# Nine merge gates of an encoder layer computed in a stage of their own ahead of the first attention, four pairs of them by seven products

## The chip, the cores and the metric

One NeuronCore of a Trainium2 chip runs the whole program. The metric is the device time of one execution in microseconds, and lower is better. The engines are TensorE (PE in the profile), VectorE (DVE), ScalarE (ACT) and GpSimd (POOL). SyncE (SP) issues the DMAs.

## The reference

Two sequences of 512 tokens (1024 tokens together, 1024 features) go through one layer. Its merge is what the change touches (`mg` is the last 3 * 1024 columns of `u`):

```python
h = rms_norm(x, pre_g)
u = h @ w_in
ya = diff_attention(...) * silu(ag)
yb = gqa_attention(...) * silu(bg)
yc = neighbourhood_attention(...) * silu(cg)
gates = jax.nn.sigmoid(mg).reshape(b, s, 3, D_MODEL)
m = gates[:, :, 0] * (ya @ wa) + gates[:, :, 1] * (yb @ wb) + gates[:, :, 2] * (yc @ wc)
x = x + rms_norm(m @ w_out, post_g)
x = x + sigmoid(x @ w_pg) * (p_i @ w_pe)
```

The gates depend on h alone, so they may be computed at any time after h is there.

## The kernel before

Features lie on the partitions and tokens along the free axis. Every product is done in float32 with each operand split into a high and a low part (`_hi`, `_lo`) and three matmuls (hi by hi, hi by lo, lo by hi). The high part of a weight is cast by ScalarE (`split_w`, line 1598 of the profile). Its low part is the difference, which GpSimd takes (line 728).

The program goes through: normalising x and turning it into h; attention A; merge 0; attention B; merge 1; attention C; merge 2; the output projection; the embedding. A merge `b` works on eight chunks `f` of 128 output features. For every chunk there is a **gate**, a product of h with 128 columns of `w_gates` (48 matmuls of 512 columns), and a **branch**, a product of the attention's output y with a block of `w_branch` (24 matmuls). ScalarE takes the tanh of the gate from PSUM into `s_row(c)` (`merge_tanh`, line 1818), and VectorE multiplies it with the branch product and adds that to `m` (`merge_add`, `add_quarter`).

Chunks 0 and 1 of a merge are done plainly. From chunk 2 on the branch products of two chunks, 2p and 2p+1, are done together as **pair p**, with seven products in place of eight (Strassen's scheme in Winograd's form, six matmuls for each product: `pair_first` does four of them, 24 matmuls, and `pair_rest` three, 18 matmuls). Merge 2 does its last two chunks plainly. VectorE puts the seven products together (`pair`, lines 2357 and 2348 to 2351). GpSimd makes the sums of the weights in place in `stage` (lines 747 to 757).

The order on each engine is written out by hand. Semaphores count up: `w_ready` the weights whose low part is done, `block_done` the weights that TensorE has used up, `mg_tanh` the gates that have been through tanh, `merged` the chunks that have gone into `m`. An engine takes its instructions strictly in the order written. TensorE's order in a merge is gate 0, gate 1, branch 0, gate 2, branch 1, gate 3, and then for each pair

```python
pair_first(b, p, n + 4 * p + 2, slot)
merge_gate(b, 2 * p + 2, n + 4 * p + 3, 1 - slot, 0)
pair_rest(b, p, n + 4 * p + 4, slot)
merge_gate(b, 2 * p + 3, n + 4 * p + 5, 1 - slot, 1)
```

with the last pair of merges 0 and 1 without gates. `pair_first` begins with `pe.wait_ge(merged, LEAD + b * KC + 2 * p)`: both chunks of the previous pair must have gone into `m`.

Of the kernel before, what the change touches and what calls it, by code (L numbers as in the profile page):

```python
# [144 lines left out]
N_MERGE = [19, 42, 74]  # L145
PAIRS = [range(1, KC // 2), range(1, KC // 2), range(1, KC // 2 - 1)]
HALF_K = 2 * P
N_B = 35
N_C = 58
N_OUT = 90  # L150
EARLY = KC - 2
N_PG = [N_OUT + 2, N_OUT + KC + 4]
N_PE = N_OUT + KC + 2

# [7 lines left out]
def build_program(nc, w_qkvg_a, w_qg_b, w_qkvg_c, w_gates, w_branch, w_out, w_pg, w_pe,  # L162
# [3 lines left out]
    with ExitStack() as ctx:  # L166
# [17 lines left out]
        m = sb("m", [P, TILES, KC, P])  # L184
# [9 lines left out]
        pt_lo = sb("pt_lo", [P, 2, QT, SEQ], F32R)  # L194
# [35 lines left out]
        x_in = [sem(f"x_in{i}") for i in range(TILES)]  # L230
# [99 lines left out]
        xr_in = [sem("x_again0"), sem("x_again1")]  # L330
        mt_hi_done = sem("mt_hi_done")
        mt_ready = sem("mt_split")
        out_w_in = [sem(f"w_out_in{k}") for k in range(EARLY)]
# [18 lines left out]
        o_stored = [sem("stored0"), sem("stored1")]  # L352
# [24 lines left out]
        FIRST_BANKS = {("q", 0): 4, ("k", 0): 5, ("q", 1): 0, ("k", 1): 1}  # L377
# [164 lines left out]
        def _(sp):  # L542
# [11 lines left out]

            def load_merge_rest(b):
                n = N_MERGE[b]
                for f in range(2):
                    load_w(n + 2 + 2 * f, n % 2, w_branch[b * KC + f])
                    load_w(n + 3 + 2 * f, (n + 1) % 2, w_gates[b * KC + 2 + f])
                for p in PAIRS[b]:  # L560
                    sp.wait_ge(w_ready, LEAD + n + 4 * p + 1)
                    pair = w_branch[b * KC + 2 * p:b * KC + 2 * p + 2].rearrange("a p n -> p a n")
                    sp.dma_start(stage[:, n % 2, :].rearrange("p (a n) -> p a n", a=2), pair) \
                        .then_inc(w_in_slot[n % 2], 16)
                    if p < KC // 2 - 1:
                        load_w(n + 4 * p + 3, (n + 1) % 2, w_gates[b * KC + 2 * p + 2])
                        sp.wait_ge(w_ready, LEAD + n + 4 * p + 3)
                        sp.sem_inc(w_in_slot[n % 2], 16)
                        load_w(n + 4 * p + 5, (n + 1) % 2, w_gates[b * KC + 2 * p + 3])
                    else:  # L570
                        sp.wait_ge(w_ready, LEAD + n + 14)
                        sp.sem_inc(w_in_slot[(n + 1) % 2], 16)
                        sp.wait_ge(w_ready, LEAD + n + 16)
# [10 lines left out]
            def load_x(t):  # L584
                sp.dma_start(x_row(t), x_tok[t]).then_inc(x_in[t], 16)
# [7 lines left out]
            sp.wait_ge(x_in[2], 16)  # L593
# [15 lines left out]
            for c in range(2):  # L609
                sp.sem_inc(o_stored[c], LEAD)  # L610
# [7 lines left out]
            for n in range(2, 4):  # L618
                load_w(N_A + n, n % 2, w_qkvg_a[N_A + n])
# [7 lines left out]
            load_w(N_KQV + 2, 0, w_qkvg_a[N_KQV + 2])  # L627

# [38 lines left out]
            for k in range(EARLY):  # L667
                sp.dma_start(out_early[k], w_out[k]).then_inc(out_w_in[k], 16)
# [4 lines left out]
            for c in range(2):  # L673
                sp.dma_start(y[:, c, :], x_tok[c]).then_inc(xr_in[c], 16)
# [23 lines left out]
            for c in range(2):  # L698
                sp.wait_ge(o_stored[c], LEAD + 16 * TILES)
# [3 lines left out]
        def _(pool):  # L703
# [18 lines left out]
            def split_w(n, slot, dst=None, width=TOK, hi=None, staged=None):  # L722
# [2179 lines left out]
```

## Time and profile before

| what | value |
|---|---|
| runs listed | 1332.16, 2647.54 and 3365.67 us |
| median of them | 2647.54 us |
| profiled execution: span | 1330.3 us |
| fastest listed run, the one that belongs beside this span | 1332.16 us (1.9 us more than the span) |
| instructions in the trace | 17488 |
| TensorE busy | 1312.1 us, 99% |
| VectorE, ScalarE, GpSimd busy | 680.8, 575.5, 352.0 us |
| HBM read and written | 66.86 and 4.23 MB |

An execution with this span cannot have taken 2647 us, so the profile describes the fastest of the three. Matmuls are pipelined: a matmul of 512 columns is shown with 0.39 us, but the next one starts 0.23 us behind it, so durations of groups in the chain of work are used, not the mean of one matmul.

### The profile page before, as it was taken

The numbers are of one execution on the slowest core, as the hardware profiler recorded it, in microseconds if no ns is written. First come the engines' busy times: TensorE is split into PE (matmuls) and PEld (weight loads), VectorE is DVE, ScalarE is ACT, GpSimd is POOL, SyncE is SP. The second block draws the span as 40 slices with busy tenths as digits, with TensorE's granted clock in tenths as the row PEclk, the third lists the DMA queues.
The fourth block names the chain that finished last, engine by engine and source line by source line (L and its number), as shares of the span: only waits on it lengthen the run. The fifth ranks groups of instructions, "written<-read, shape, count | busy, mean of one in ns | idle before, by whom it ended". The sixth has DMA issues, their size and how long they took to land.

```text
span 1330.3 us, 17488 instructions
## 1 busy us (share of the span) xinstructions
PE 1312.1 (99%) x6636; PEld 1072.0 (81%) x6636; DVE 680.8 (51%) x1285; ACT 575.5 (43%) x1106; POOL 352.0 (26%) x239
## 2 busy tenths in 40 slices
PE   8999999999999999999999999999999999999998
PEld 6788877888888778788888888888877888888887
DVE  6354655556522677786633435555557337435222
ACT  6355455553222577676422245555554223223210
POOL 4122212222434311130244512221211443213100
PEclk9999999999999999999999999999999999999999
DMA  6111112111111200000111211111001114422111
GB/s 214 63 41 41 46 36 57 52 32 52 49 48 32 67 30 16 17 20 21 52 52 32 81 61 33 51 51 42 32 24 41 48 40 167 140 81 70 58 40 40
DMA packets 25712, 72.18 MB, mean 54 GB/s; under 512 B 2808, under 2 KB 4728, under 8 KB 25504
## 3 DMA queue, kind: packets, MB, share of 16 engines
q1 hardware_dynamic: 25632, 71.09, 16.9%
q8 instruction: 53, 0.87, 0.3%
q14 instruction: 27, 0.22, 0.1%
HBM read 66.86 MB, written 4.23 MB: 53 GB/s over the span
## 4 chain that ended last, share of the span: by engine, by line
PE 90%; DVE 4%; ACT 3%; issue 1%; DMA 1%; POOL 1%; SPq 0%; ACTq 0%; DVEq 0%; POOLq 0%
PE ps L934 18%; PE ps L953 14%; PE ps L1290 13%; PE ps L1548 7%; PE ps L1528 6%; PE ps L1175 5%; PE ps L1342 5%; PE ps L1331 2%; PE ps L973 2%; PE ps L1112 2%; PE ps L1028 2%; PE ps L1260 2%; PE ps L1554 2%; PE ps L1406 2%; PE ps L1143 1%; PE ps L1234 1%
## 5 line engine op out<-in xcount | busy, mean ns | idle before, releaser
L728 POOL TENSOR_TENSOR w_lo<-stage,w_hi 128x1024 fp32r<-128x1024 f32 (+2 forms) x84 | 190.3, 2265 | 577.5 <-ACT w_hi L1598 577.5
L1598 ACT CAST w_hi<-stage 128x1024 fp32r<-128x1024 f32 (+2 forms) x92 | 91.3, 992 | 198.0 <-PE ps L934 125.9
L2148 DVE TENSOR_TENSOR pt_lo<-ps,pt_hi 128x512 fp32r<-128x512 f32 (+2 forms) x160 | 97.1, 607 | 80.6 <-ACT pt_hi L1962 40.3
L953 PE MATMUL ps<-h_hi,w_hi 128*128 128x512 f32 x272 | 110.3, 405 | 0.0
L934 PE MATMUL ps<-h_hi,w_hi 128*128 128x512 f32 x352 | 108.9, 391 | 0.7 <-POOL w_lo L728 0.7
L934 PE MATMUL ps<-h_lo,w_hi 128*128 128x512 f32 x352 | 108.5, 389 | 0.0
L934 PE MATMUL ps<-h_hi,w_lo 128*128 128x512 f32 x352 | 108.4, 389 | 0.0
L1290 PE MATMUL ps<-h_hi,w_hi 128*128 128x512 f32 x256 | 106.8, 417 | 0.0
L953 PE MATMUL ps<-h_hi,w_lo 128*128 128x512 f32 x272 | 106.2, 391 | 0.0
L953 PE MATMUL ps<-h_lo,w_hi 128*128 128x512 f32 x272 | 106.1, 390 | 0.0
L1290 PE MATMUL ps<-h_hi,w_lo 128*128 128x512 f32 x256 | 100.5, 392 | 0.0
L1290 PE MATMUL ps<-h_lo,w_hi 128*128 128x512 f32 x256 | 100.3, 392 | 0.0
L709 POOL TENSOR_TENSOR small<-small 128x1 f32<-128x1 f32 (+3 forms) x32 | 34.2, 1067 | 174.2 <-DVE small L2163 173.5
L934 PEld LDWEIGHTS ps<-h_hi,w_hi 128*128 128x128 f32 x352 | 65.6, 188 | 15.1 <-issue 1.8
L934 PEld LDWEIGHTS ps<-h_hi,w_lo 128*128 128x128 f32 x352 | 66.1, 188 | 13.8
L934 PEld LDWEIGHTS ps<-h_lo,w_hi 128*128 128x128 f32 x352 | 66.1, 188 | 13.8
L953 PEld LDWEIGHTS ps<-h_hi,w_hi 128*128 128x128 f32 x272 | 51.1, 188 | 15.1 <-issue 5.4
L1627 ACT ACTIVATE s<-s,stat 128x512 f32<-128x512 f32 x64 | 45.8, 716 | 38.0 <-DVE stat L2199 38.0
L1175 PE MATMUL ps<-h_hi,w_hi 128*128 128x512 f32 x144 | 59.8, 415 | 0.5 <-POOL w_lo L728 0.5
L953 PEld LDWEIGHTS ps<-h_hi,w_lo 128*128 128x128 f32 x272 | 51.1, 188 | 11.2
L953 PEld LDWEIGHTS ps<-h_lo,w_hi 128*128 128x128 f32 x272 | 51.2, 188 | 9.3
L2470 DVE CUSTOM_DVE_ANT_0 s<-ps,tables_plain 128x256 f32<-128x256 f32 (+1 forms) x64 | 29.0, 489 | 56.2 <-PE ps L1234 51.9
(386 smaller groups left out, 3059.3 us busy)
## 6 DMA issues: line engine op xcount, KB each, us to landing
stage<-in_w_gates SPq DMA_DIRECT2D x24, 512.0 KB, 3.6
stage<-in_w_qkvg_a SPq DMA_DIRECT2D x19, 512.0 KB, 4.4
stage<-in_w_qkvg_c SPq DMA_DIRECT2D x16, 512.0 KB, 3.6
m<-in_x_tok SPq DMA_DIRECT2D x8, 512.0 KB, 6.4
stage<-in_w_branch SPq DMA_DIRECT2D x8, 512.0 KB, 3.7
y_plain<-in_x_tok SPq DMA_DIRECT2D x8, 512.0 KB, 3.7
stage<-in_w_pg SPq DMA_DIRECT2D x16, 256.0 KB, 3.0
out<-y_plain SPq DMA_DIRECT2D x16, 256.0 KB, 2.0
```

Of the source, the lines that this page charges most:

```text
L709: nc.gpsimd.tensor_tensor(dst, src, neg_half.broadcast_to([P, n]), ALU.pow).then_inc(signal, 1)
L728: nc.gpsimd.tensor_tensor(dst, stage[:, staged, 0:width], f32(hi), ALU.subtract).then_inc(w_ready, 1)
L934: done = mm(ps[:, bank + g, :], w[:, slot, k * P:(k + 1) * P], h[:, k, g * SEQ:(g + 1) * SEQ], start=first and part == 0, stop=last and pa ...
L953: done = mm(ps[:, half_bank(T), :], w[:, slot, k * P:(k + 1) * P], h[:, k, g * SEQ:(g + 1) * SEQ], start=k == 0 and part == 0, stop=k == K ...
L1175: done = mm(ps[:, bank_b(name, unit, g), :], w[:, slot, k * P:(k + 1) * P], h[:, k, g * SEQ:(g + 1) * SEQ], start=k == 0 and part == 0, st ...
L1290: done = mm(ps[:, bank, :], w[:, slot, k * P:(k + 1) * P], h[:, k, g * SEQ:(g + 1) * SEQ], start=k == 0 and part == 0, stop=k == KC - 1 an ...
L1342: done = mm(ps[:, bank, :], w[:, slot, cols], h[:, c, :], start=c == 0 and part == 0, stop=c == 1 and part == 2)
L1528: done = mm(ps[:, 2 * c + nb, :], a[:, k * P:(k + 1) * P], w[:, k, nb * 512:(nb + 1) * 512], start=k == 0 and part == 0, stop=k == KC - 1 ...
L1548: mm(ps[:, c, :], a[:, k * P:(k + 1) * P], w[:, k * 512:(k + 1) * 512], start=k == 0 and part == 0, stop=k == KC - 1 and part == 2)
L1598: nc.scalar.copy(dst, stage[:, staged, 0:width]).then_inc(w_hi_done, 1)
L1627: done = nc.scalar.activation(probs, probs, ACT.Exp, bias=stat[:, T % 2, 2 + e:3 + e], accum_out=stat[:, T % 2, 4 + e:5 + e])
L2148: sub = lambda out, whole, hi: nc.vector.tensor_tensor(out, whole, f32(hi), ALU.subtract)
```

## The change

The odd gates from 3 to 7 of the three merges, nine of 24, move into a stage of their own, between the first projections and attention A. Gate 3 of merge 0 is done plainly (`plain_gate`, two halves of 24 matmuls). The other eight form four pairs, each done by seven products of 12 matmuls (`gate_product`). The sums of h that the scheme needs are made once: two of the four whole copies by GpSimd, all the rest by VectorE. ScalarE casts the high parts and takes the tanh. Each quarter of a gate pair, 128 by 512, is stored to DRAM (`gate_scratch`), and the merge loads the row of 128 by 1024 back into `s_row(1)` when it needs it (`load_gate_row`).

In a merge the order on TensorE becomes gate 0, gate 1, branch 0, branch 1, gate 2, and then for each pair `pair_first`, gate 2p+2, `pair_rest`. The core of the diff (`merge` is ScalarE's part, `gate_w_sums` and `gate_adds` are VectorE's):

```diff
+            def load_gate_row(b, f):
+                sp.wait_ge(merged, LEAD + b * KC + f - 1)
+                sp.dma_start(s_row(1), gate_scratch[b * KC + f]).then_inc(row_in[1], 16)
...
             def load_merge_rest(b):
...
                 if KC // 2 - 1 not in PAIRS[b]:
                     for f in range(2):
-                        load_w(n + 14 + f, (n + f) % 2, w_branch[b * KC + 6 + f])
+                        load_w(n + 11 + f, (n + 11 + f) % 2, w_branch[b * KC + 6 + f])
+                    load_gate_row(b, 7)
+                    sp.wait_ge(w_ready, LEAD + n + 12)
+                    sp.sem_inc(w_in_slot[(n + 11) % 2], 16)
...
             def merge_rest(b):
-                merge_gate(b, 2, n + 3, 1 - slot, 0)
-                merge_branch(b, 1, n + 4, slot)
-                merge_gate(b, 3, n + 5, 1 - slot, 1)
+                merge_branch(b, 1, n + 3, (n + 1) % 2)
+                merge_gate(b, 2, n + 4, n % 2, 0)
                 for p in PAIRS[b]:
...
-                        merge_gate(b, 2 * p + 2, n + 4 * p + 3, 1 - slot, 0)
-                        pair_rest(b, p, n + 4 * p + 4, slot)
-                        merge_gate(b, 2 * p + 3, n + 4 * p + 5, 1 - slot, 1)
+                        merge_gate(b, 2 * p + 2, at + 1, 1 - slot, 0)
+                        pair_rest(b, p, at + 2, slot)
...
+            def gate_product(J, product):
+                a, a22 = G_A1, G_A22[J % 2]
+                (s2s4, s3s1) = G_S
+                (hi, lo), first, state = {P1: (a, 0, "11"), P2: (a, SEQ, "21"), P3: (s2s4, SEQ, "22"), P6: (s2s4, 0, 2),
+                                          P7: (s3s1, 0, 3), P5: (s3s1, SEQ, 1), P4: (a22, 0, 4)}[product]
+                gate_bank_free(7 * J + product)
...
+                for c in range(QT):
+                    cols = slice(first + c * P, first + (c + 1) * P)
+                    for part, (w, h) in enumerate([(hi, 0), (hi, 1), (lo, 0)]):
+                        done = mm(ps[:, g_bank(J, product), :], w[:, cols], G_STATE[state][h][:, c, :],
+                                  start=c == 0 and part == 0, stop=c == QT - 1 and part == 2)
...
+            plain_gate(0)
             first_product("q", 1, range(KC))
             first_product("k", 1, range(KC))
+            plain_gate(1)
+            for J in range(N_PAIRS):
+                for product in range(7):
+                    gate_product(J, product)
+            pe.wait_ge(g_added, 7 * N_PAIRS - 4)
             half_step(-2, lambda T: None)
+            pe.wait_ge(g_tanh, GROUPS + 4 * N_PAIRS)
             score_pair(0)
...
             def merge(b):
-                split_w(n + 3, 1 - slot, uses(3))
                 merge_tanh(b, 1, n + 1, 1)
-                split_w(n + 4, slot, uses(4), width=512)
+                split_w(n + 3, (n + 1) % 2, uses(n + 3), width=512)
+                split_w(n + 4, n % 2, uses(n + 4))
...
-                split_w(n + 5, 1 - slot, uses(5))
-                merge_tanh(b, 2, n + 3, 0)
+                merge_tanh(b, 2, n + 4, 0)
                 for p in PAIRS[b]:
                     pair(p)
...
+            def gate_w_sums(J):
+                a11, a12, a21, a22 = [G_RAW[J % 2][:, q * SEQ:(q + 1) * SEQ] for q in range(4)]
+                steps.done(dve, nc.vector.tensor_tensor(a22, a21, a22, ALU.add))
+                nc.vector.tensor_tensor(a21, a11, a21, ALU.subtract)
+                steps.done(dve, nc.vector.tensor_tensor(a11, a22, a11, ALU.subtract))
+                nc.vector.tensor_tensor(a12, a12, a11, ALU.subtract).then_inc(gw_summed, 1)
...
+            for J in range(N_PAIRS):
+                gate_adds(J)
```

Three places show how the rows move.

**TensorE, merge 1, where pair 1 ends and pair 2 begins.** Before, the last six matmuls of the pair (line 1342) are followed by gate 5 (line 934):

```order
L1342 MATMUL ps<-pt_hi,w_hi 128x512 [waits second_partial_saved]
L1342 MATMUL ps<-pt_lo,w_hi 128x512
L1342 MATMUL ps<-pt_hi,w_lo 128x512
L1342 MATMUL ps<-pt_hi,w_hi 128x512
L1342 MATMUL ps<-pt_lo,w_hi 128x512
L1342 MATMUL ps<-pt_hi,w_lo 128x512
L934 MATMUL ps<-h_hi,w_hi 128x512 [waits w_split,merge_tanh_done]
L934 MATMUL ps<-h_hi,w_hi 128x512
L934 MATMUL ps<-h_lo,w_hi 128x512 x2
```

In the changed kernel the same six (now line 1454) are followed at once by the first product of pair 2, which waits for `merged`:

```order
L1454 MATMUL ps<-pt_hi,w_hi 128x512 [waits second_partial_saved]
L1454 MATMUL ps<-pt_lo,w_hi 128x512
L1454 MATMUL ps<-pt_hi,w_lo 128x512
L1454 MATMUL ps<-pt_hi,w_hi 128x512
L1454 MATMUL ps<-pt_lo,w_hi 128x512
L1454 MATMUL ps<-pt_hi,w_lo 128x512
L1454 MATMUL ps<-pt_hi,w_hi 128x512 [waits w_split,merged]
L1454 MATMUL ps<-pt_lo,w_hi 128x512
L1454 MATMUL ps<-pt_hi,w_lo 128x512
L1454 MATMUL ps<-pt_hi,w_hi 128x512
```

Gate 5, 48 matmuls, has gone from between them.

**ScalarE, merge 1, from the sums of y to the weights of pair 1.** Line 1861 (2026 after) casts the sums, the 128x1024 casts of line 1598 (1766) are high parts of weights, line 1818 (1986) is a tanh and line 1831 (2000) belongs to pair 1. Before:

```order
L1861 CAST y<-y_plain 128x2x512
L1861 CAST q_hi<-q_lo_plain 128x1024
L1598 CAST w_hi<-stage 128x1024 [waits block_done,stage1_in]
L1818 ACTIVATE s<-ps 128x1024 [waits merged,block_done]
L1598 CAST w_hi<-stage 128x1024 [waits block_done,stage0_in]
L1831 CAST pt_hi<-k_hi_plain 128x512 x2
L1834 CAST w_hi<-stage 128x256 [waits weight_sums_done]
```

In the changed kernel:

```order
L2026 CAST y<-y_plain 128x2x512
L2026 CAST q_hi<-q_lo_plain 128x1024
L1986 ACTIVATE s<-ps 128x1024 [waits merged,block_done]
L1766 CAST w_hi<-stage 128x1024 [waits block_done,stage1_in]
L2000 CAST pt_hi<-k_hi_plain 128x512 x2
L2003 CAST w_hi<-stage 128x256 [waits weight_sums_done]
```

The cast of gate 3's weights is gone from ahead of the tanh of gate 2, so that the tanh stands next ahead of the cast of pair 1's weights, as before, but with no other gate on TensorE behind gate 2.

**SyncE, the end of merge 2.** Before, the loads of the output projection's weights (line 668) follow the two last blocks of `w_branch`:

```order
L563 DMA stage<-in_w_branch 128x2x512 [waits w_split]
L546 DMA stage<-in_w_gates 128x1024 [waits w_split] x2
L546 DMA stage<-in_w_branch 128x512 [waits w_split] x2
L668 DMA y_plain<-in_w_out 128x1024 [waits max_ready,state_sums_done,y_written,y_split]
L668 DMA y_plain<-in_w_out 128x1024 x3
L668 DMA vg_plain<-in_w_out 128x1024
L668 DMA tables_plain<-in_w_out 128x1024
```

In the changed kernel the load of a gate row (line 619) has come between, and waits for `merged`:

```order
L607 DMA stage<-in_w_gates 128x1024 [waits w_split]
L619 DMA s<-gate_scratch 128x1024 [waits merged]
L607 DMA stage<-in_w_branch 128x512 [waits w_split] x2
L619 DMA s<-gate_scratch 128x1024 [waits merged]
L777 DMA y_plain<-in_w_out 128x1024 [waits w_split,max_ready,state_sums_done,y_written,y_split]
L777 DMA y_plain<-in_w_out 128x1024 x3
L777 DMA vg_plain<-in_w_out 128x1024
```

## Rows read from the trace of the kernel before

**Rows 1.** The page: busy time and share of TensorE, and its granted clock.

```profile
PE 1312.1 (99%) x6636; PEld 1072.0 (81%) x6636; DVE 680.8 (51%) x1285; ACT 575.5 (43%) x1106; POOL 352.0 (26%) x239
...
PEclk9999999999999999999999999999999999999999
```

**Rows 2.** Waits of TensorE: total us, times, longest.

```profile
PE ps L1112 <- DVE pt_lo L2148: 2.8, 8, 0.6
...
PE ps L934 <- POOL w_lo L728: 0.7, 1, 0.7
```

**Rows 3.** Chain that ended last, in merges 0 and 1: start, us, what.

```profile
357.57 10.88 PE ps L934 x48
368.45 5.44 PE ps L1342 x24
...
384.77 4.13 PE ps L1342 x18
388.90 10.89 PE ps L934 x48
...
664.37 10.88 PE ps L934 x48
...
691.57 4.08 PE ps L1342 x18
695.65 10.88 PE ps L934 x48
```

**Rows 4.** Timeline of ScalarE, merge 0, around the weights of pair 1: start, us, what.

```profile
353.18 1.02 ACT L1818 ACTIVATE s<-ps 128x1024 f32<-128x1024 f32 x1
357.66 1.05 ACT L1598 CAST w_hi<-stage 128x1024 fp32r<-128x1024 f32 x1 [3.47 <-PE ps L1331]
...
362.37 0.41 ACT L1834 CAST w_hi<-stage 128x256 fp32r<-128x256 f32 x1 [2.61 <-POOL stage L748]
```

**Rows 5.** Timeline of GpSimd at the same weights, merge 0 and (last row) merge 1.

```profile
358.79 2.40 POOL L747 TENSOR_TENSOR w_lo<-stage,w_hi 128x1024 fp32r<-128x1024 f32 x1 [3.04 <-ACT w_hi L1598]
361.26 1.07 POOL L748 TENSOR_TENSOR stage<-stage 128x256 f32<-128x256 f32 x1
362.92 0.74 POOL L751 TENSOR_TENSOR w_lo<-stage,w_hi 128x256 fp32r<-128x256 f32 x1 [0.59 <-ACT w_hi L1834]
...
670.25 1.17 POOL L751 TENSOR_TENSOR w_lo<-stage,w_hi 128x256 fp32r<-128x256 f32 x1 [0.58 <-ACT w_hi L1834]
```

**Rows 6.** Timeline of VectorE behind pair 1 of merge 0.

```profile
390.99 1.88 DVE L2348 SCALAR_TENSOR_TENSOR m<-s,ps 128x512 f32<-128x512 f32 x3
```

**Rows 7.** Timeline of VectorE behind pair 1 of merge 1.

```profile
698.49 1.34 DVE L2351 TENSOR_TENSOR m<-m,s 128x512 f32<-128x512 f32 x1
...
701.79 0.69 DVE L2351 TENSOR_TENSOR m<-m,s 128x512 f32<-128x512 f32 x1
```

**Rows 8.** Timelines of the end of merge 2: SyncE, ScalarE, TensorE.

```profile
1100.07 1.75 SPq L668 DMA_DIRECT2D y_plain<-in_w_out  x4
...
1112.48 3.88 ACT L2076 CAST h_hi<-y_plain 128x1024 fp32r<-128x1024 f32 x4
...
1121.66 0.62 PE L1528 MATMUL ps<-h_hi,q_hi 128*128 128x512 f32 x2
```

**Rows 9.** DMA issues between 1090 and 1140 us: median us to landing.

```profile
y_plain<-in_w_out SPq DMA_DIRECT2D x4, 512.0 KB, 7.3
```

**Rows 10.** Timelines of the first 30 us: VectorE and GpSimd.

```profile
19.09 1.28 DVE L2399 SCALAR_TENSOR_TENSOR m<-m,small,vg_plain 128x1024 f32<-128x1024 f32 x1
21.14 3.40 DVE L2399 SCALAR_TENSOR_TENSOR m<-m,small,vg_plain 128x1024 f32<-128x1024 f32 x1 [0.78 <-POOL small L709]
...
21.07 2.39 POOL L728 TENSOR_TENSOR w_lo<-stage,w_hi 128x1024 fp32r<-128x1024 f32 x1
```

**Rows 11.** Timeline of TensorE at the start of the program.

```profile
1.45 6.83 PE L920 MATMUL ps<-pt_hi 128*128 128x512 f32 x20 [1.45 <-DVE pt_hi L2150]
...
11.03 1.64 PE L920 MATMUL ps<-pt_hi 128*128 128x512 f32 x6
```

More of the change, by code:

```diff
@@ L153 @@
 N_PE = N_OUT + KC + 2
+GATE_PLAIN = (0, 3)
+GATE_PAIRS = [((0, 5), (0, 7)), ((1, 3), (1, 5)), ((1, 7), (2, 3)), ((2, 5), (2, 7))]
+N_PAIRS = len(GATE_PAIRS)
+GATE_RING = [6, 7, 4, 5, 0, 1, 2, 3]
+P1, P2, P3, P6, P7, P5, P4 = range(7)
+QUARTERS = [(0, 0), (1, 1), (0, 1), (1, 0)]
+GATE_SLOTS = 4
+GATES_STORED = [len(range(slot, GROUPS + 4 * N_PAIRS, GATE_SLOTS)) for slot in range(GATE_SLOTS)]
+TANHS = [0, 1, 2, 4, 6]
+ROWS_BACK = 9
 KEPT = 6
@@ L627, in _ @@
             load_w(N_KQV + 2, 0, w_qkvg_a[N_KQV + 2])
+            for slot in range(GATE_SLOTS):
+                sp.wait_ge(o_stored[slot], 16 * GATES_STORED[slot])
             sp.wait_ge(maxed, LEAD + TILES)
@@ L787, in _ @@
                 x_inv_sqrt(t)
+            pool.wait_ge(gw_hi_done, 1)
+            nc.gpsimd.tensor_tensor(G_PLAIN[1], stage[:, 0, :], f32(G_PLAIN[0]), ALU.subtract).then_inc(gp_ready, 1)
+            pool.wait_ge(h_ready, LEAD + QT)
+            for T, half in ((1, 0), (4, 1)):
+                hi, lo = h_quarter(half, 0)
+                nc.gpsimd.tensor_tensor(G_SUM[T], f32(hi), f32(lo), ALU.add).then_inc(gt_whole, 1)
             spread_bias(0)
@@ L1361, in pair_first, with pair_rest @@
                 pair_product(slot, 2 * HALF_K, T_PARTS[b][1], 3).then_inc(block_done, 1)
[L1363 removed]
+            def pair_rest(b, p, n, slot, count=1):
                 number = pair_number(b, p)
@@ L1393, in merge_rest, with plain_gate @@
                 if KC // 2 - 1 not in PAIRS[b]:
-                    merge_branch(b, 6, n + 14, slot)
-                    merge_branch(b, 7, n + 15, 1 - slot)
+                    merge_branch(b, 6, n + 11, (n + 11) % 2)
+                    merge_branch(b, 7, n + 12, (n + 12) % 2, count=2)
+            def plain_gate(g):
+                hi, lo = G_PLAIN
+                pe.wait_ge(gp_ready, 1)
+                if g == 0:
+                    pe.wait_ge(h_ready, LEAD + 6)
+                bank = [0, 3][g]
+                for k in range(KC):
+                    for part, (w, h) in enumerate([(hi, h_hi), (hi, h_lo), (lo, h_hi)]):
+                        done = mm(ps[:, bank, :], w[:, k * P:(k + 1) * P], h[:, k, g * SEQ:(g + 1) * SEQ],
+                                  start=k == 0 and part == 0, stop=k == KC - 1 and part == 2)
+                done.then_inc(gate_half, 1)
@@ new lines, in gate_adds @@
+            def gate_adds(J):
+                x0, x1 = G_X
+                more = J + 1 < N_PAIRS
+                bank = lambda product: ps[:, g_bank(J, product), :]
+                add = lambda out, in0, in1: nc.vector.tensor_tensor(out, in0, in1, ALU.add).then_inc(g_added, 1)
+                if more:
+                    gate_a22_lo(J + 1)
+                dve.wait_ge(g_p1_saved, J + 1)
+                dve.wait_ge(g_done, 7 * J + 2)
+                add(bank(P2), x0, bank(P2))
+                if more:
+                    gate_a1_lo(J + 1)
+                    gate_w_sums(J + 1)
+                dve.wait_ge(g_done, 7 * J + 4)
+                add(x0, x0, bank(P6))
+                if more:
+                    gate_sum_lo(J + 1, 0)
+                dve.wait_ge(g_done, 7 * J + 5)
+                dve.wait_ge(g_added, 7 * J + 2)
+                add(x1, x0, bank(P7))
+                dve.wait_ge(g_done, 7 * J + 6)
+                add(x0, x0, bank(P5))
+                dve.wait_ge(g_added, 7 * J + 3)
+                add(bank(P5), x1, bank(P5))
+                dve.wait_ge(g_added, 7 * J + 4)
+                add(bank(P3), x0, bank(P3))
+                dve.wait_ge(g_done, 7 * J + 7)
+                add(bank(P4), x1, bank(P4))
+                if more:
+                    gate_sum_lo(J + 1, 1)
@@ L2432, in _ @@
+            gate_sum_lo(0, 1)
+            gate_state_lo(1)
+            gate_state_lo(4)
+            for J in range(N_PAIRS):
+                gate_adds(J)
             dve.wait_ge(const_in, 16 * 3)
```

437 lines of the change are left out of this document (323 added, 114 removed).

## The prediction, made before the changed kernel ran

> **What bounds the kernel now.** I read the page first. TensorE is busy for 1312.1 of the 1330.3 us and its granted clock is full all along; no other engine is above 51% [rows 1]. Then the waits of TensorE: the largest sum is 2.8 us, and the only wait on a low part of a merge's weights is 0.7 us [rows 2]. So the kernel is a string of matmuls, and an edit is worth what it removes from the string or what gap it opens in it. Last I read the chain that ended last through merges 0 and 1. It is TensorE from end to end, gate and pair parts butted together: 10.88 us for a gate, 5.44 for 24 matmuls of a pair, 4.13 for 18 [rows 3]. That is 0.2267 us for a matmul of 512 columns. What the other engines do under each gate is then read in the timelines of ScalarE, GpSimd and VectorE.
>
> Of the runs listed, only 1332.16 fits the profiled span (1.9 us more). I make the sum against it; the median, 2647.54, is of executions that this profile does not describe. Two per cent, about what a measurement of this kernel can tell from no change, is 26.6 us.
>
> **Matmuls removed.** Nine gates of 48 matmuls are 432. In their place come one plain gate of 48 and four pairs of 7 x 12 = 84, together 384. 48 fewer at 0.2267 give **-10.9 us**. Two small waits go: the 0.7 us on GpSimd's low part [rows 2], whose weights get time while the new stage runs, and some 0.5 us (an estimate) where the first projections waited for the last of h, since the plain gate's first half needs less of it. Together **-12.1**.
>
> **The entrance of pair 1, three merges.** After the change TensorE has nothing between gate 2 and pair 1. What pair 1 needs is seen in merge 0: the cast of its weights on ScalarE (1.05 us at 357.66), GpSimd's low part 2.40, its sums 1.07, a cast of 0.41, GpSimd's 0.74, done at 363.66 [rows 4, 5]. Gate 3 ran from 357.57 to 368.45 [rows 3] and hid the 6.1 us. The order on ScalarE now puts the tanh of gate 2, 1.02 us [rows 4], ahead of that cast, and the tanh cannot begin before gate 2 has ended. So the wait is 6.1 + 1.0 = 7.1 us. In merge 1 the same chain ran from 664.37 to 671.42 [rows 3, 5], 7.05 without the tanh; GpSimd's short operations were longer there, beside VectorE's adds of branch 1. These adds now fall under gate 2, so I take 7.1 in all three: **+21.3**, with 18 and 24 as ends.
>
> **Behind `pair_rest`, six places.** `pair_first` of the next pair, and in merge 2 branch 6, waits until both chunks of the pair are in `m`. Before, the odd gate ran meanwhile. In merge 0 the matmuls of pair 1 ended at 388.90 [rows 3] and VectorE's last operation on it at 390.99 + 1.88 = 392.87 [rows 6]: 3.97 us. In merge 1 they ended at 695.65 [rows 3] and VectorE at 701.79 + 0.69 = 702.48 [rows 7]: 6.83, because gate products must be multiplied and then added to `m` instead of set. One add there took 1.34 where its like took 0.69 [rows 7], so 0.65 is a collision with GpSimd; GpSimd's work on the next weights will shift, and I take 6.2. Two waits of merge 0 at 4.0, two of merge 1 and two of merge 2 at 6.2: **+32.8**, ends 26 and 37. Nothing late behind these: the weights of the next pair need about the 6 us of rows 4 and 5, beginning when `pair_first` has freed their slot, and lie under the even gate.
>
> **The exit of merge 2.** SyncE issued the loads of the output projection at 1100.07 [rows 8], just as pair 2 ended; call that T. They landed 7.3 us later [rows 9]. ScalarE's four casts began at T + 12.4 and TensorE went on with the projection at T + 21.6 [rows 8], behind gate 7 and two branches, with no wait to speak of. Now the load of gate row 7 stands ahead of them in SyncE's queue and waits for `merged`, T + 6.2, and its 512 KB are in the same queue: four such loads took 7.3 [rows 9], so at most 1.8 for one; I take 1.4. The projection's loads land at T + 6.2 + 1.4 + 7.3 = T + 14.9. TensorE, without gate 7, is through both branches at T + 6.2 + 10.9 = T + 17.1. The first cast (1.0) and the low parts, of which VectorE did four in one run of some 4.6 us, with one more operation of about 1 us ahead of what TensorE needs, reach T + 21.5. That is a wait of 4.4, and for the load's own issue 0.4 each on SyncE (1.75 for four, [rows 8]) I take **+5**, ends 2 and 8.
>
> **The new stage.** Gates now go out to DRAM in 16 stores of 256 KB and come in again in 8 loads of 512 KB. A row is asked for when the pair before is in `m`, and used 5.4 + 10.9 + 4.1 = 20 us later [rows 3]; even the 7.3 us of rows 9 lie under that, so nothing. VectorE is the risk. Per pair it has 12 additions of 128x512 at 0.69 [rows 7] and three of 128x1024 at 1.22 to 1.28 [rows 10], 12 us, ScalarE 6.5, against 84 matmuls, 19.0 us: covered by 7 us. The first pair also needs the sums of h: some ten operations twice as wide as the 1.28 of rows 10, about 24 us, from 1.0 us after TensorE enters the stage until P3, which TensorE reaches after 120 matmuls, 27.2 us. If they run freely there is 2 us in hand. But a VectorE operation of 1.28 took 3.40 while GpSimd's of 2.39 ran [rows 10], and GpSimd makes two of the copies here: if the first sum is so held, VectorE is 4.4 us later and TensorE waits 2.3. I take **+1.5**, ends 0 and 20 (the upper end: each pair short by 5 us, where every 1024-wide addition meets GpSimd as in rows 10). The Trainium skill, "GPSIMD Engine Reference", in its table of the engine, says that GpSimd shares its SBUF interfaces with VectorE and that an instruction of VectorE with two SBUF inputs contends for them; by that the first sum is held and the wait is 2.3, without it 0.
>
> The sum so far: 1332.2 - 12.1 + 21.3 + 32.8 + 5 + 1.5 = **1380.7**.
>
> **How TensorE goes on after a gap.** The trace of before has no gap above 1.5 us, so it has no row for a restart but the start of the program: its first 20 matmuls took 6.83 us where 20 x 0.2267 is 4.5 [rows 11], and later ones have their usual rate. That is 2.3 us lost, though the granted clock of the page reads full in that slice too [rows 1]. Seven of the waits (three of 7.1, four of 6.2) are long; if each ends in such a restart, 7 x 2.3 = **+16.1**; the bounds are 0 and 7 x 2.3 with the two waits of 4 us as well, 20.7. I take 16.1, as the start of the program is the only gap of this length that I can see. The Trainium skill, "TensorE: Matmul & The Clock Gate", in its section on why this matters for kernels, says that an idle gap between bursts of matmuls puts the clock back to half of full speed, 1.2 of 2.4 GHz; by that rule each such wait would be paid for twice, which speaks against this change more than its own waits do. No wait of the trace can show it.
>
> The forecast is 1380.7 + 16.1 = **1397** (1396.8).
>
> **The rivals.**
> (1) *The waits without slow restarts*: matmuls run at full rate at once after a gap, 1381. For it: no gate in the chain shows such a price. Against it: none stands behind a long wait, and [rows 11] is the one stretch that does.
> (2) *The waits are short, the other side*: the chains behind gate 2 and behind `pair_rest` shrink, since VectorE and GpSimd work alone while TensorE stands still, and reading PSUM meets no matmuls. The place is the nine merge waits, the price their mean. The time is 1332.2 - 12.1 + 5 + 1.5 = 1326.6 plus nine waits; it stays under the 2% line at 1358.8 when they hold less than 32.2 us, 3.6 us each, against 6.0 by the rows. With 2.8 each it is 1352 (1351.8). With fully covered waits, were an order on an engine other than I read it, it would be 1321, the 10.9 us gained, which is also less than 2%. Against it: operations like 128x512 at 0.69 hold their length in every row without a collision.
> (3) *The new stage starves TensorE*: 20 us more as above, and four more slow starts at most: 1415 or so. For it: the 3.40 us row. Against it: GpSimd has little to do in the stage after the first pair.
> (4) *The change doesn't do what it says*: the order of the instructions shows that the nine gates left the merges, so this is nearly out.
>
> **How the numbers follow.** The forecast of 1397 has 0.50; rival 1 (1381) 0.27; rival 3 (1415) 0.10; rival 2 within 2% (about 1352) 0.11 with the covered case in it; faster by over 2%, under 1305.5, would need more than the 10.9 us that the matmuls can give, 0.02. The predicted time is 1397. Low end: rival 1 with the waits at their low ends (18 for 21.3, 26 for 32.8, 2 for 5) is 1367.6, 1368. High end: the forecast with its entrance and tail terms at 24 and 37 and the exit at 8 is 1407, and the larger restarts and part of rival 3 carry it to 1414. What is left out is rival 2 and half of rival 3, under 0.2. Chances: faster 0.02, same 0.11, slower 0.87.
>
> **What the changed profile would show.** The string of matmuls: 6488 instead of 6536 in all, and no gate between `pair_rest` and the next `pair_first`. The waits of TensorE: three of about 7 us on GpSimd's second low part, and six of 4 to 6.5 on VectorE's adds; if these are under 3.6 us on average, rival 2 holds. The first matmuls behind each: a group of 24 at 7.7 us instead of 5.44 shows the slow restart, 5.44 rival 1. In the exit: the six loads issued some 7 us after `pair_rest`'s end and a wait of about 5 before the output projection. In the new stage: a wait of 0 to 2.3 us ahead of the first P3 and none in later pairs; waits of several us in each pair show rival 3. I would be wrong outright if the weights of pair 1 or the adds were let go at another point than the orders show, or if the time between the new stage and attention A were not hidden by its last products.

## The result, and the profile after

The changed kernel takes 1412.49 us (median of four runs, 1411.8 to 1413.84). The ratio to the kernel before is **1.060** (95% interval 1.059 to 1.062). Left out of every comparison are executions far above the rest of their kernel: 2647.54 and 3365.67 us of the kernel before here, for which no clock is on record, and later one of 1449.52 us of that kernel and one of 1438.69 us of the first experiment's, both at a lower granted clock. The other two of the kernel before here are 1332.16 and 1332.57 us. The change is **80 us slower**. The forecast was 1397, 65 us slower, with a range from 1368 to 1414.

The page's engine line, the granted clock, and then the waits of TensorE in the changed kernel (who waits for whom: total us, times, longest), which answer to [rows 1, 2]:

```profile
PE 1325.7 (94%) x6588; PEld 1078.9 (77%) x6588; DVE 752.3 (53%) x1355; ACT 593.1 (42%) x1131; POOL 341.6 (24%) x233
...
PEclk9999999999999989999998989999999989999999
```

```profile
PE ps L1454 <- POOL w_lo L853: 21.0, 3, 7.0
PE ps L1454 <- DVE m_plain L2597: 18.8, 3, 6.4
PE ps L1443 <- DVE m_plain L2597: 7.1, 1, 7.1
PE ps L1285 <- POOL w_lo L837: 4.1, 2, 3.6
PE ps L1071 <- ACT s L1986: 4.0, 1, 4.0
PE ps L1454 <- DVE m_plain L2594: 4.0, 1, 4.0
PE ps L1044 <- POOL w_lo L837: 3.7, 1, 3.7
...
PE ps L1696 <- DVE m_plain L2556: 2.8, 1, 2.8
```

TensorE still has by far the most work, but it now stands still for 84.3 us of the span (1410.0 less 1325.7), 66 more than before (18.2), and the clock row has four 8s where it had only 9s. Three rows were forecast by name: the low part of pair 1's weights (three times 7.0), the adds of the pair before (18.8, 4.0 and 7.1 in five waits, and 4.0 where the third pair of merge 0 waits for a tanh), and the exit of merge 2 (2.8). Two were not: 3.6 and 3.7 us for a low part at L1285 and L1044, the first products of attentions B and C.

The chain that ended last, from the end of gate 2 of merge 0 into attention B (start, us, what):

```profile
435.70 10.89 PE ps L1044 x48
...
446.64 0.90 issue
447.54 1.05 ACT w_hi L1766
448.65 2.35 POOL w_lo L849
451.08 1.06 POOL stage L850
452.16 0.41 ACT w_hi L2003
452.71 0.73 POOL w_lo L853
...
453.58 7.04 PE ps L1454 x24
...
479.66 7.36 PE ps L1454 x24
...
508.01 11.10 PE ps L1454 x42
519.18 1.05 ACT w_hi L1766
520.31 2.36 POOL w_lo L837
522.71 8.22 PE ps L1285 x24
```

Read against [rows 3 to 5], the gate that stood over these short steps is gone. The 0.90 us called issue is the time in which ScalarE runs the tanh of gate 2; behind it come the same five steps as before, now on the path. Then look at the groups behind each gap: 24 matmuls took 7.04, 7.36 and 8.22 us, where 24 took 5.44 before. The windows around the first gap and around the one at the exit show the clock (start:end, us, busy of TensorE, its weight loads, VectorE, ScalarE, GpSimd, then the granted clock, DMA share, GB/s):

```profile
435.70:446.58 10.88, 10.88 (x49) 8.67 (x47) 5.76 (x5) 0.00 (x0) 1.05 (x1) 1.00 0.24 83
446.58:453.58 7.00, 0.00 (x1) 0.03 (x1) 3.03 (x2) 4.34 (x6) 4.12 (x3) 0.71 0.00 0
453.58:457.00 3.42, 3.42 (x9) 2.74 (x10) 0.00 (x0) 0.48 (x1) 3.33 (x3) 0.59 0.00 0
...
1198.85:1201.60 2.75, 0.00 (x0) 0.03 (x1) 2.71 (x4) 2.41 (x3) 0.07 (x1) 1.00 0.07 27
1201.60:1205.00 3.40, 3.40 (x15) 2.81 (x16) 3.40 (x2) 0.40 (x1) 3.40 (x2) 1.00 0.00 0
```

The clock falls within the gap of 7.00 (0.71 of full speed over the gap), and the first 3.4 us of matmuls behind it run at 0.59 on average: nine are begun where 15 are begun behind the gap of 2.75, which cost nothing of the clock. Most of that stretch lies at the lower of the two levels, 1.2 GHz, where the matmuls start 0.427 us apart instead of 0.227. So a long gap is paid for twice.

What the first part of the program costs is read from where attention A begins, ahead of its first group of 24 matmuls; before and then after (two fences of the chain):

```profile
45.59 5.44 PE ps L953 x24
```

```profile
63.56 71.00 PE ps L1554 x312
134.56 5.44 PE ps L1063 x24
```

It begins 88.97 us later, 1.9 more than the stage's 384 matmuls (87.05). One wait of 1.6 stands ahead of P3, the third product, of the first pair, and from there 312 matmuls run in 71.00 us, 0.2276 each: in the other pairs nothing waits.

The time between the two profiled executions, 1410.0 - 1330.3 = 79.7 us, is then:

| term | forecast | measured |
|---|---|---|
| matmuls removed, 48 | -10.9 | -10.9 |
| waits in the first part (stage, start) | +1.0 | +1.9 |
| entrance of pair 1, three | +21.3 | +21.0 |
| behind `pair_rest`, six (4.03, 4.04, 6.24, 6.40, 6.20, 7.07) | +32.8 | +34.0 |
| exit of merge 2 | +5.0 | +2.8 |
| starts of B and C (3.62, and 3.72 for 0.67) | -0.7 | +6.7 |
| slow matmuls behind gaps | +16.1 (seven) | +25.1 (eleven) |
| sum | +64.6 | +80.6 |

The last measured term is the sum of what each group behind a gap took over its like in the kernel before: 1.6, 1.9, 2.6, 2.8, 2.7, 1.8, 2.8, 1.4, 3.0, 1.9 and 2.5 us, 2.28 on average. (The sum is 0.9 over the difference of the spans; small waits elsewhere moved too.)

### The profile page after: what moved, and what is told of

It reads as the page before. It is cut to its first block, busy times and chain, and to the rows that moved or that the text cites. A ratio compares the mean times of both kernels' runs of the same rounds, so it can differ in the third digit from the quotient of the medians.

```text
span 1410.0 us, 17557 instructions
## 1 busy us (share of the span) xinstructions
PE 1325.7 (94%) x6588; PEld 1078.9 (77%) x6588; DVE 752.3 (53%) x1355; ACT 593.1 (42%) x1131; POOL 341.6 (24%) x233
## 4 chain that ended last, share of the span: by engine, by line
PE 84%; DVE 8%; ACT 3%; issue 2%; DMA 1%; POOL 1%; SPq 0%; DVEq 0%; ACTq 0%; POOLq 0%
PE ps L1063 13%; PE ps L1400 12%; PE ps L1044 10%; PE ps L1716 6%; PE ps L1454 6%; PE ps L1285 6%; PE ps L1696 6%; PE ps L1554 5%; PE ps L1443 2%; PE ps L1083 2%; PE ps L1222 2%; PE ps L1138 2%; PE ps L1370 2%; PE ps L1722 2%; PE ps L1253 1%
## 5 line engine op out<-in xcount | busy, mean ns | idle before, releaser
L837 POOL TENSOR_TENSOR w_lo<-stage,w_hi 128x1024 fp32r<-128x1024 f32 (+2 forms) x75 | 168.7, 2251 | 587.4 <-ACT w_hi L1766 587.4
L1766 ACT CAST w_hi<-stage 128x1024 fp32r<-128x1024 f32 (+2 forms) x83 | 81.4, 984 | 116.8 <-PE ps L1044 55.5
L1063 PE MATMUL ps<-h_hi,w_hi 128*128 128x512 f32 x272 | 110.3, 405 | 0.0
L1400 PE MATMUL ps<-h_hi,w_hi 128*128 128x512 f32 x256 | 106.8, 417 | 0.0
L1063 PE MATMUL ps<-h_hi,w_lo 128*128 128x512 f32 x272 | 106.3, 391 | 0.0
L1063 PE MATMUL ps<-h_lo,w_hi 128*128 128x512 f32 x272 | 106.1, 390 | 0.0
L1400 PE MATMUL ps<-h_hi,w_lo 128*128 128x512 f32 x256 | 100.5, 392 | 0.0
L1400 PE MATMUL ps<-h_lo,w_hi 128*128 128x512 f32 x256 | 100.3, 392 | 0.0
L1454 PE MATMUL ps<-pt_hi,w_hi 128*128 128x512 f32 x60 | 30.9, 514 | 43.8 <-POOL w_lo L853 21.0
L1044 PE MATMUL ps<-h_hi,w_hi 128*128 128x512 f32 x208 | 65.1, 394 | 3.7 <-POOL w_lo L837 3.7
L1285 PE MATMUL ps<-h_hi,w_hi 128*128 128x512 f32 x144 | 60.9, 423 | 4.1 <-POOL w_lo L837 4.1
L1044 PE MATMUL ps<-h_lo,w_hi 128*128 128x512 f32 x208 | 64.5, 392 | 0.0
L1044 PE MATMUL ps<-h_hi,w_lo 128*128 128x512 f32 x208 | 64.5, 391 | 0.0
L1063 PEld LDWEIGHTS ps<-h_hi,w_hi 128*128 128x128 f32 x272 | 51.1, 188 | 15.1 <-issue 5.4
L1063 PEld LDWEIGHTS ps<-h_hi,w_lo 128*128 128x128 f32 x272 | 51.1, 188 | 11.2
L1063 PEld LDWEIGHTS ps<-h_lo,w_hi 128*128 128x128 f32 x272 | 51.2, 188 | 9.3
L2434 DVE CUSTOM_DVE_ANT_0 s<-ps,m_plain 128x512 f32<-128x512 f32 x48 | 31.2, 688 | 50.1 <-PE ps L1118 35.8
L1285 PE MATMUL ps<-h_hi,w_lo 128*128 128x512 f32 x144 | 57.4, 399 | 0.0
```

Source lines behind the costliest of these rows:

```text
L837: nc.gpsimd.tensor_tensor(dst, stage[:, staged, 0:width], f32(hi), ALU.subtract).then_inc(w_ready, count)
L1044: done = mm(ps[:, bank + g, :], w[:, slot, k * P:(k + 1) * P], h[:, k, g * SEQ:(g + 1) * SEQ], start=first and part == 0, stop=last and pa ...
L1063: done = mm(ps[:, half_bank(T), :], w[:, slot, k * P:(k + 1) * P], h[:, k, g * SEQ:(g + 1) * SEQ], start=k == 0 and part == 0, stop=k == K ...
L1285: done = mm(ps[:, bank_b(name, unit, g), :], w[:, slot, k * P:(k + 1) * P], h[:, k, g * SEQ:(g + 1) * SEQ], start=k == 0 and part == 0, st ...
L1400: done = mm(ps[:, bank, :], w[:, slot, k * P:(k + 1) * P], h[:, k, g * SEQ:(g + 1) * SEQ], start=k == 0 and part == 0, stop=k == KC - 1 an ...
L1454: done = mm(ps[:, bank, :], w[:, slot, cols], h[:, c, :], start=c == 0 and part == 0, stop=c == 1 and part == 2)
```

## The experiments

All start from the changed kernel. Measured beside them, the kernel before took 1332.2 to 1332.4 us (medians).

**Tanh behind the cast.** In ScalarE's order in each merge:

```diff
-                merge_tanh(b, 2, n + 4, 0)
                 for p in PAIRS[b]:
                     pair(p)
...
-                    if p > 1:
-                        merge_tanh(b, 2 * p, at - 2, 0)
+                    merge_tanh(b, 2 * p, at - (2 if p > 1 else 1), 0)
```

> The tanh of gate 2 goes behind the cast of pair 1's weights on ScalarE, in all three merges. Theory: the three waits of 7.0 us ahead of pair 1 go (21.0 us), and with them the slow matmuls behind them (a group of 24 took 7.04, 8.18 and 8.48 instead of 5.44: 7.4 us together). 1412.5 - 28.4 = 1384, between 1382 and 1388. Rival A, the slow matmuls belong to the start of pair 1 and not to the wait: only 21 us go, 1391. Rival B, what holds pair 1 is also something else (the sums of y, the adds of branch 1): waits of more than 2 us stay and the time is above 1395.

Measured: 1389.1 us, 23.4 less, ratio 1.043 (1.041 to 1.045), just above the expected range. The waits of TensorE there, and then a row of its chain, pair 1 of merge 0:

```profile
PE ps L1454 <- DVE m_plain L2595: 18.8, 3, 6.4
...
PE ps L1454 <- POOL w_lo L853: 2.6, 2, 1.3
...
PE ps L1696 <- DVE m_plain L2554: 2.0, 1, 2.0
```

```profile
445.60 5.44 PE ps L1454 x24
```

The row of 21.0 us is now 2.6 (1.3 in merges 1 and 2, where two short steps of GpSimd take 1.6 and 1.79 us beside VectorE's work, for 1.06 and 0.73 in the changed kernel). Between the two profiled executions lie 23.8 us: 20.3 are time in which TensorE stood still, 18.4 of them in this row, and 3.5 are busy time, that is, less slow matmuls. I had put 7.4 there: the three restarts went, but others came out longer than in the changed kernel, and the shorter wait at the exit, 2.0 us, was now followed by slow matmuls (1.4 us lost) where 2.75 before had cost none. Nothing else held pair 1: rival B is out. The time lies close to rival A's 1391, but the chain speaks against it: with no wait left ahead of it, pair 1 of merge 0 takes 5.44 us instead of 7.04. The next run tests the same with the waits kept.

**Filling the waits.** Matmuls that nobody reads, in banks that are free:

```diff
+            def fill(b, count):
+                for i in range(count):
+                    mm(ps[:, gate_bank(b, 1) + i % 2, :], y_hi[:, 0:P], y_hi[:, 0:SEQ], start=True, stop=True)
...
                 for p in PAIRS[b]:
...
+                    if p == 1:
+                        pe.wait_ge(merged, LEAD + b * KC + 2)
+                        fill(b, 28)
+                    else:
+                        fill(b, 15 if b == 0 else 25)
...
+                if KC // 2 - 1 in PAIRS[b]:
+                    fill(b, 14)
                 if KC // 2 - 1 not in PAIRS[b]:
+                    fill(b, 28)
```

> Matmuls of 512 columns whose product nobody reads are put into eleven waits (28 ahead of pair 1, 15 in merge 0's and 25 in the others' waits behind pair_rest, 14 behind the last pair of merges 0 and 1, 28 ahead of branch 6), each group somewhat shorter than the wait. Theory, the slow restart is the price of TensorE having been idle: the granted clock stays at full, each group of 24 behind a wait takes 5.44 and the waits with their filling are as long as before: 25 us less, 1387, between 1384 and 1393. Rival, the first matmuls behind a wait are slow for what they read or write there: no gain, 1412 or more.

Measured: 1392.9 us, ratio 1.046 (1.044 to 1.048). The windows over the first gap and behind it (columns as above), then the chain behind it:

```profile
446.60:453.00 6.40, 5.67 (x26) 4.42 (x25) 3.10 (x2) 3.62 (x6) 4.27 (x4) 1.00 0.00 0
453.00:458.00 5.00, 5.00 (x23) 4.13 (x24) 1.38 (x2) 0.59 (x1) 4.47 (x4) 1.00 0.31 77
```

```profile
452.91 5.69 PE ps L1454 x24
...
477.64 5.73 PE ps L1454 x24
```

The chains that hold TensorE are as long as before (gate 2's end to pair 1 is 7.0 us still), the clock stays at 1.00 in these windows, and the groups take 5.69 and 5.73 in place of 7.04 and 7.36. So the loss behind the gaps belongs to TensorE's idleness, not to what pair 1 reads; the rivals that said otherwise are out. It gained 19.6 of the 25 us. Of the rest, 3.1 is in the exit, where I had put no fill: there the wait was 4.3 us instead of 2.8, and was followed by a restart of 1.5.

```profile
PE ps L1709 <- DVE m_plain L2569: 4.3, 1, 4.3
```

The wait grew because the branches ahead of it got faster. From the first load of `w_out` on SyncE's queue TensorE was through both branches after 10.7 us (1165.84 to 1176.51), where the changed kernel, with the restart of 2.5 behind its wait ahead of branch 6, had needed 12.8 (1186.02 to 1198.85); the projection could begin 15.0 us behind that load, and 15.6 in the changed kernel. So a restart had hidden a part of the exit's wait. What is left of the 25 us, some 2.3, is by my estimate in the groups behind the filled waits, which still take 0.25 to 0.3 us more than 5.44.

**A finer wait.** `pair_first` writes banks 0 and 1 first, and the tail reads banks 2 and 3 last:

```diff
-                pe.wait_ge(merged, LEAD + b * KC + 2 * p)
+                pe.wait_ge(merged, LEAD + b * KC + 2 * p - (1 if p > 1 else 0))
...
                 pair_product(slot, HALF_K, plain_state(1, 0), 1).then_inc(product_done, 1)
+                pe.wait_ge(merged, LEAD + b * KC + 2 * p)
```

> pair_first waits for one chunk of the pair before where it waited for two, and for the second ahead of its third product. Theory: four operations of VectorE (2.7 us) of the tail come to lie under the first two products of pair 2 and 3 in merges 1 and of pair 2 in merge 2, 1.3 us in merge 0's pair 2; merge 0's pair 3 waits for a tanh and is unchanged. 3 x 2.7 + 1.3 = 9.4 us less, and where the wait that is left is under 3 us no slow restart, 1.9 more: 1401 to 1403. Rival, the weights or the third product's wait take the place: 1407 or more.

Measured: 1404.95 us, ratio 1.055 (1.053 to 1.056). Its waits, and then the windows over the gap in merge 0 and behind it:

```profile
PE ps L1454 <- DVE m_plain L2598: 10.9, 3, 3.8
...
PE ps L1454 <- DVE m_plain L2595: 2.8, 1, 2.8
```

```profile
476.90:479.70 2.80, 0.00 (x0) 0.00 (x0) 2.73 (x6) 0.41 (x1) 1.01 (x2) 1.00 0.00 0
479.70:483.00 3.30, 3.29 (x8) 2.64 (x9) 1.15 (x2) 2.30 (x3) 1.22 (x1) 0.51 0.27 94
```

The waits fell by 7.9 and 1.2 us, as expected (9.4). The time fell by 7.5, not by 11, and TensorE's busy time rose by 1.8 us (1327.5 for 1325.7): my guess that a wait under 3 us pays no restart was wrong. This one of 2.8 was followed by one, at 0.51 of full speed, while the 2.75 at the exit of the changed kernel was not. The length of the gap alone does not decide it; what does is open.

**The w_out loads first.**

```diff
-                    load_gate_row(b, 7)
...
             for k in range(EARLY):
                 sp.dma_start(out_early[k], w_out[k]).then_inc(tile_in[k], 16)
+            load_gate_row(2, 7)
...
+            sp.wait_ge(merged, LEAD + 3 * KC)
```

> The load of gate row 7 of merge 2 goes behind the four w_out loads on SyncE's queue (and the loads of x wait until all chunks are merged). Theory: the wait of 2.75 us ahead of the output projection goes, nothing else: 1409 to 1410. Rival, that wait is of VectorE's own work: no change, 1412.

Measured: 1409.95 us, ratio 1.058 (1.056 to 1.060). The row of 2.8 us ahead of the output projection is gone from the waits and 2.5 us from the time. So the queue on SyncE did hold the exit.

**High parts first at the starts of B and C.** The two first products took high and low parts in turn for each piece of the weights, and began only when GpSimd's low part was there:

```diff
-                pe.wait_ge(w_ready, LEAD + N_C + n + 1)
...
-                for k in range(KC):
-                    done = project_part(n, bank, k, k == 0, k == KC - 1)
+                if n == 0:
+                    pe.wait_ge(w_hi_done, LEAD + N_C + 1)
+                    todo = [(k, w, h) for w, h in [(w_hi, h_hi), (w_hi, h_lo), (w_lo, h_hi)] for k in range(KC)]
+                    for at, (k, w, h) in enumerate(todo):
+                        if at == 2 * KC:
+                            pe.wait_ge(w_ready, LEAD + N_C + 1)
```

> The first product of attention B and that of C take all matmuls with the high part of the weights first and wait for the low part only behind them. In the changed kernel these two began 3.6 and 3.7 us after the last pair, behind a cast and a low part of 2.4. Theory: both waits shrink by 2.4 to 1.2 and 1.3, 4.8 us, and the slow matmuls behind them (2.7 and 1.4 us) go or shrink: 1404 to 1408. Rival, the slow restart comes whatever the length: 1407.7.

Measured: 1402.97 us, ratio 1.053 (1.051 to 1.055). The start of B in its chain:

```profile
519.17 1.05 ACT w_hi L1784
520.27 5.78 PE ps L1294 x24
```

The waits are 1.19 and 1.28 and no restart follows (5.78 where it was 8.22). 9.5 us went, a little over the 8.9 that I had as the most, so the time is just below the expected range. It confirms the two unforeseen terms, 3.6 and 3.7, and that each drew a slow stretch behind it.

**Half gates.** The even gate is split in two, and the second half takes the place of the odd gate behind `pair_rest`; all pairs' weights use the slot that `pair_rest` leaves. With it go the three edits above on the tanh, the finer wait and the w_out loads:

```diff
-                        merge_gate(b, 2 * p + 2, at + 1, 1 - slot, 0)
+                        half_gate(b, 2 * p + 2, at + 1, 1 - slot, 0)
                         pair_rest(b, p, at + 2, slot)
+                        half_gate(b, 2 * p + 2, at + 1, 1 - slot, 1)
```

> The even gate behind each pair_first is split: one half (24 matmuls) stays there, the other goes behind pair_rest, and the next pair's weights take the slot that pair_rest leaves. With it the tanh of gate 2 behind the cast, pair_first's finer wait, and the w_out loads first. Theory: 5.4 us of matmuls cover the tail of VectorE (3.5 to 4.8) and nearly the weights' 6.1; what is left of the nine merge waits is 0 to 1.3 us each, without slow restarts. Without any wait and restart the changed kernel would take 1412.5 - 61.6 - 25.1 - 2.8 = 1323; with 2.6 at the entrances, about 0.9 at five places, 1.1 for the turn in merge 0 and the two unchanged starts of B and C (6.6 and 4.1) it is 1342, between 1337 and 1350. Rival, a chain that I don't see (the weights of pair_rest, ready only some 10 us behind pair_first's start) takes their place: above 1360.

Measured: 1342.57 us, ratio 1.0075 (1.0057 to 1.0092). Its chain in merge 1 from pair 1's end to pair 2:

```profile
740.66 4.09 PE ps L1456 x18
744.84 1.06 ACT w_hi L1783
745.96 2.42 POOL w_lo L851
748.45 1.08 POOL stage L852
749.55 0.42 ACT w_hi L2020
750.10 0.74 POOL w_lo L855
750.98 5.69 PE ps L1456 x24
```

From 744.58 to 750.18 the second half of the gate runs, which is why this chain of 6.2 us costs only 0.8 at the end. 70 of the 80 us are back, without one of the nine gates returning to the merges. So what the change cost was mainly cover (work of TensorE under which the other engines' steps are hidden), not the stage. The run has four edits at once; three of them gained 23.4, 7.5 and 2.5 us by themselves, so some 37 us are the half gates' and that of the restarts that go with the last long waits.

**All of it.** Half gates, high parts first, and the turn of the rope buffer in merge 0 into other banks:

```diff
-                        pe.wait_ge(mg_tanh, LEAD + gate_tanhs(b, 6))
-                        turn(rope_buf, 4, rope_turned)
+                        turn(rope_buf, 6, rope_turned)
```

> All of these: half gates, cast first, finer wait, w_out loads first, high parts first at the starts of B and C, and in merge 0 the turn of the rope buffer into other banks of PSUM, where it need not wait for a tanh. Theory: 1342 less 4.8 and 4.1 at B and C and less 1.0 for the turn: 1332, between 1328 and 1338, so about the kernel before, since what is left of waits (9 us) eats the 10.9 us of matmuls. Rival, the nine gates' removal is itself not worth 10.9 us: above 1340.

Measured: 1332.48 us, ratio 1.000 (0.999 to 1.001). This kernel took the low part of attention B's first queries from the banks used before, so that part of its computation is not the reference's. With that low part taken from the new banks:

```diff
-            merge(0, between=lambda: rope_scale(1), before_6=lambda: q_to_lo(UNITS, 4))
+            merge(0, between=lambda: rope_scale(1), before_6=lambda: q_to_lo(UNITS, 6))
```

> As e10_all, with the low part of B's first queries read from the same banks as their high part (in e10_all it was left at the old ones, so its output differed there). Nothing of the order on TensorE changes: 1332.5, between 1331.5 and 1333.5.

Measured: 1331.89 us, ratio 0.9998 (0.9989 to 1.0007). TensorE stands still for 27.2 us of the span, where before it was 18.2, which eats most of the 10.9 us of matmuls. The waits that the kernel before doesn't have:

```profile
PE ps L1464 <- POOL w_lo L855: 5.4, 6, 1.3
...
PE ps L1578 <- DVE w_lo L2420: 1.6, 1, 1.6
...
PE ps L1687 <- ACT w_hi L1800: 1.3, 1, 1.3
PE ps L1296 <- ACT w_hi L1800: 1.2, 1, 1.2
```

**The pairs without their weights' sum.** The first row of these waits is for the sum of the weights, which the first three products do not read:

```diff
-                pe.wait_ge(w_ready, LEAD + n + 1)
+                pe.wait_ge(w_summed, LEAD + 2 * pair_number(b, p) + 1)
                 pair_product(slot, 0, plain_state(0, 0), 0).then_inc(product_done, 1)
...
+                pe.wait_ge(w_ready, LEAD + n + 1)
                 pair_product(slot, 2 * HALF_K, T_PARTS[b][1], 3)
```

> As e11_all_rope, and pair_first begins when the low part of the pair's own weights is there; the sum of the weights (a cast of 0.41 and a GpSimd operation of 0.74 to 1.8 later) is waited for ahead of the fourth product, the only one that reads it. Theory: the seven waits of 0.4 to 1.3 us on GpSimd at pair_first, 5.8 us together, go: 1326.7, between 1325.5 and 1329, about 0.4% below the kernel before. Rival, the adds of VectorE or the fourth product's own wait stand right behind them: 1330 or more.

Measured: 1328.33 us, ratio **0.997** (0.996 to 0.998) to the kernel before, the only version below it, by 4 us, and 1.6 behind the 1326.7 expected. The gain is clear of the interval but small, 0.3%. The row of 5.4 us is gone; 0.9 of it came back as a wait for a low part and 1.3 as one for VectorE's adds:

```profile
PE ps L1464 <- DVE m_plain L2589: 1.3, 2, 0.7
```

## Why the prediction fell short

**Right, and measured.** The matmuls: 432 have left the merges and 384 stand in the stage, 6588 on the page for 6636 before (the prediction's 6488 and 6536 are each 100 too low, their difference is right). The entrance of pair 1: 21.0 for 21.3, by the five steps of [rows 4, 5] and the tanh ahead of them, and moving that tanh gave 18.4 of it back. The collision of merge 1 in [rows 5] (1.17 for 0.74) went, as taken. The six waits behind `pair_rest`: 34.0 for 32.8; merge 0's were 4.03 and 4.04 for 4.0. The exit of merge 2 had the right cause (the loads behind the gate row in SyncE's queue), but its term, 5, measured 2.8, since TensorE came to it late behind a restart of 2.5; in the run with filled waits it was 4.3, for the 4.4 of the prediction. The stage: a wait of 1.6 for 1.5. VectorE's two first sums took 9.19 us together while GpSimd made its own, and one like them took 2.28 without it, so they were held by 4.6 us (4.4 in the prediction, which made a wait of 2.3 of it); the 1.5 was a value between that and none, and that it fits is luck. VectorE kept up in the later pairs, so rival 3 is out. Rival 2, that the waits are short, is out: the nine average 6.1 us. Rival 1, no slow restarts, is out by the clock in the windows and by the filled waits.

**The step that failed first: "Nothing late behind these: the weights of the next pair need about the 6 us of rows 4 and 5 ...".** I looked for what is late behind the last gates only as far as the next pair. Behind the third pair of merges 0 and 1 come the first products of B and C. Their weights took the slot that the last pair's `pair_rest` uses: a pair now takes three numbers of the weights' count instead of four, and the slot follows the number's parity. So ScalarE's cast began at 519.18, when the last pair had ended at 519.11, and 1.05 + 2.36 us and the handing over between engines stood on the path. Before, in merge 1, that wait was the 0.7 of [rows 2], and I even counted it as gained ("the 0.7 us on GpSimd's low part"). Together 7.4 us were missing. All of it could be read from the order of the instructions and the slots before any run.

**The step that failed second: "Seven of the waits (three of 7.1, four of 6.2) are long".** The price of a restart was right on average: 2.28 where I took 2.3 from [rows 11], one row that stood for prices from 1.4 to 3.0. The count was wrong. I left the two waits of 4.0 out of the forecast and kept them only for the range, and had not seen the two at B and C; all four were followed by slow matmuls (1.9, 2.6, 2.8, 1.4 us, 8.7 together). The term measured 25.1 for 16.1, 9.0 more. These two steps, 7.4 and 9.0, less the exit's 2.2 make 14.2 of the 16.0 us between the sums of the table; the waits behind `pair_rest` have 1.2 more, the first part 0.9, the entrances 0.3 less.

That 1412.5 lies within the range is luck for the most part. Its top was made of entrances of 24, tails of 37, an exit of 8 and a part of rival 3, and these came to 21.0, 34.0, 2.8 and a stage that kept up; only the restarts behind the waits of 4.0 were among what carried the time up there. The low parts at B and C were in no bound.

Which of the short gaps draw a restart stays open. In these runs gaps of 2.0 and 2.8 us were followed by slow matmuls, and others of 2.1 (in the run with half gates), 2.3 (in the run with the finer wait), 2.7 and 2.75 were not. That all eleven gaps of the changed kernel from 3.6 us up did is what the rows show, and no more.

The Trainium skill's sentence in "TensorE: Matmul & The Clock Gate", in the section on why this matters for kernels, that an idle gap between bursts of matmuls puts the clock back to half, is borne out by the granted clock of 0.59 and 0.51 behind gaps, and by 1.00 in the windows where they were filled; but not every gap did it, as the 1.00 behind the one of 2.75 us shows.

## What to carry to other kernels

Ahead of taking work off the bounding engine, list for each piece what the other engines do while it runs, to the end of the following stage: a gate of 10.9 us covered 7 us of small steps, and shortening the gates' arithmetic by 1.2 us each was paid with their cover. What comes free is spent best by splitting what is left (a half gate on each side) and by waiting only for what the next instruction reads; here this brought a loss of 80 us to a gain of 4, or 0.3%. Where buffers alternate by a count, a change of the count's parity changes which slot the next stage waits for, so follow the count past the code that was edited.

## What the runs showed of the hardware that I had not expected

Behind a gap the loss varies between 1.6 and 3.0 us for the same 24 matmuls, and from run to run at the same place (the gap of 7.00 ahead of pair 1 in merge 0 cost 1.6 us in the changed kernel and 3.0 in the run with the finer wait). A gap of 2.8 us was followed by 1.9 us of loss (7.31 for 5.44), where one of 2.75 lost none.

The granted clock can also fall only when TensorE has already gone on. In the changed kernel, behind the gap of 4.03 ahead of pair 2 of merge 0:

```profile
479.66:480.20 0.54, 0.54 (x2) 0.48 (x3) 0.00 (x0) 0.54 (x1) 0.00 (x0) 1.00 0.00 0
480.20:483.00 2.80, 2.80 (x8) 2.19 (x7) 0.00 (x0) 0.85 (x2) 2.46 (x2) 0.51 0.57 187
```

Two matmuls start at the full clock, and the following ones at about half. So a clock of 1.00 up to the end of a gap does not show that the gap is free. While TensorE stood still in merges 1 and 2, the chains of VectorE behind `pair_rest` took 6.20 to 6.40 us (7.07 ahead of branch 6, where the last add took 1.57), the 6.83 of [rows 7] less the collision of 0.65 there: its operations of 0.69 us got no faster by TensorE leaving PSUM alone.
